# Moving the sample rows' normalisation and half of chunk 1's projection inside a retention head

## What is computed

```python
h = rmsnorm(x, g_mix)
u, q, k, v, ga, gb = jnp.split(h @ w_in, IN_SPLITS, axis=-1)
pool_out, new_hist = pool_mixer(u, pool_hist, pool_valid, w_pool, pool_scale)
qf = rotary(q, pos); kf = rotary(k, pos) * RET_DK ** -0.5
ret, s_new = retention(qf, kf, v, ret_state)          # 4 heads, chunks of 128 rows
ret_out = head_group_norm(ret, ret_gn)                # (o - mean) * rsqrt(var + EPS) per row and head
mixed = sigmoid(ga) * pool_out + sigmoid(gb) * ret_out
x = x + mixed @ w_out
x = x + hier_moe(rmsnorm(x, g_ffn))                   # 32 experts, two for each row
```

## Time and profile before

| | us |
|---|---|
| median of 3 runs (1114.18 to 1115.68) | 1114.87 |
| the profiled execution, whole | 1117.15 |
| its span, first to last instruction | 1115.0 |
| PE busy in the span | 1018.3 (91%) |
| DVE busy in the span | 758.4 (68%) |
| ACT busy in the span | 441.9 (40%) |
| mean granted TensorE clock | 0.965 |

### The profile page before, as it was taken

The page is one execution under the profiler, slowest core; times in us unless marked ns, Lnnn a source line. Parts: engine busy times, 40 slices in busy tenths (PEclk is TensorE's granted clock), DMA queues, the critical chain, the costliest instruction groups (busy, mean ns, idle before and its releaser), DMA issues.

```text
span 1115.0 us, 17147 instructions
## 1 busy us (share of the span) xinstructions
PE 1018.3 (91%) x5426; PEld 866.0 (78%) x5427; DVE 758.4 (68%) x1846; ACT 441.9 (40%) x733; POOL 211.3 (19%) x227
## 2 busy tenths in 40 slices
PE   5799999899998999999998999968999999998980
PEld 5788887888888888788885888856887877777860
DVE  5674556746557455574566667668998989878964
ACT  6521113011130111301112211235988888877964
POOL 0001220012200122001221000002423333345310
PEclk9899999999999999999998999988999999999995
DMA  8511016010060010610107433288999999999728
GB/s 253 201 31 55 11 40 195 2 40 28 23 194 21 24 44 13 190 34 24 44 11 259 157 134 115 113 322 346 352 384 387 377 375 361 376 361 344 244 34 311
DMA packets 74736, 190.36 MB, mean 171 GB/s; under 512 B 12504, under 2 KB 47556, under 8 KB 62228
## 3 DMA queue, kind: packets, MB, share of 16 engines
q1 hardware_dynamic: 61403, 159.66, 38.7%
q0 software_dynamic: 13248, 29.62, 9.5%
HBM read 167.43 MB, written 38.68 MB: 185 GB/s over the span
## 4 chain that ended last, share of the span: by engine, by line
PE 61%; DMA 23%; DVE 9%; issue 4%; ACT 1%; SPq 1%; POOLq 0%; POOL 0%; DVEq 0%; ACTq 0%
DMA sum_d<-y,icol 18%; PE bank L1788 16%; PE bank L1789 8%; PE bank L848 8%; PE bank L821 6%; PE bank L823 5%; PE bank L822 5%; DMA xg<-h_d,icol 2%; DVE line L1999 2%; PE bank L877 1%; PE bank L1810 1%; PE bank L1802 1%; PE bank L1798 1%; PE bank L1685 1%; DMA hc<-const_head_tables_dram 1%
## 5 line engine op out<-in xcount | busy, mean ns | idle before, releaser
L1194 DVE TENSOR_TENSOR w_lo<-w,w_hi 128x1024 fp32r<-128x1024 f32 x128 | 150.6, 1217 | 0.7 <-ACT w_hi L711 0.2
L711 ACT ACTIVATE w_hi<-w 128x1024 fp32r<-128x1024 f32 x128 | 129.5, 1068 | 4.3 <-PE bank L823 4.3
L1788 PE MATMUL bank<-wvg_hi,hT_hi 128*128 128x512 f32 x288 | 117.0, 406 | 0.0
L1638 ACT ACTIVATE v<-bank 128x256 f32<-128x256 f32 x36 | 13.8, 383 | 252.6 <-PE bank L1789 252.6
L1788 PE MATMUL bank<-wvg_lo,hT_hi 128*128 128x512 f32 x288 | 113.5, 394 | 0.0
L1788 PE MATMUL bank<-wvg_hi,hT_lo 128*128 128x512 f32 x288 | 113.2, 393 | 0.0
L821 PE MATMUL bank<-w_hi,xT_hi 128*128 128x512 f32 x256 | 103.8, 405 | 3.2 <-DVE xT_lo L1205 1.5
L821 PE MATMUL bank<-hT_hi,wuqk_hi 128*128 128x344 f32 x288 | 97.4, 338 | 8.7 <-DVE qT L1975 6.9
L823 PE MATMUL bank<-w_hi,xT_lo 128*128 128x512 f32 x256 | 100.9, 394 | 0.0
L822 PE MATMUL bank<-w_lo,xT_hi 128*128 128x512 f32 x256 | 100.4, 392 | 0.0
L822 PE MATMUL bank<-hT_lo,wuqk_hi 128*128 128x344 f32 x288 | 94.2, 327 | 0.0
(11 more groups left out here) (231 smaller groups left out, 2380.2 us busy)
## 6 DMA issues: line engine op xcount, KB each, us to landing
w<-in_w_dram SPq DMA_DIRECT2D x96, 1024.0 KB
raw<-in_w_in_dram SPq DMA_DIRECT2D x60, 256.0 KB, 3.2
xall<-in_x_prompt_dram SPq DMA_DIRECT2D x8, 512.0 KB, 7.1
mixed_d<-mixed POOLq DMA_DIRECT2D x32, 128.0 KB, 2.2
sample_state<-in_state_ret_dram SPq DMA_DIRECT2D x16, 256.0 KB, 3.8
out_dram<-sample_state SPq DMA_DIRECT2D x16, 256.0 KB, 3.7
mixed_in<-mixed_d SPq DMA_DIRECT2D x8, 512.0 KB, 4.4
x_again<-in_x_prompt_dram SPq DMA_DIRECT2D x8, 512.0 KB, 3.3
```

What stands on the lines that cost most here:

```text
L711: act.activation(hi, whole_w, ACT.Copy).then_inc(S["up_hi"], 1)
L1194: dve.tensor_tensor(lo, whole_w, hi, ALU.subtract).then_inc(S["up_lo"], 1)
L1788: g = pe.matmul(gates, x[xi], wvg[wi][:, 1:3, k, :], start=first, stop=last)
```

## The change

`finish(h - 1, CH)` leaves the end of `tail` and stands behind the first rotation of the next head, n = 3. `finish_rest(h - 1, CH)` moves from behind rotation 3 to behind rotation 6. Behind head 3 both keep their place. On PE, the projection of chunk 1 is cut in two: its first four k steps are issued ahead of `before(1)`, the other four behind it. The number of instructions of each kind stays the same, and no buffer changes.

```diff
-                def project(c):
-
-                    if c == 0:
-                        pe.wait_ge(S["w_lo"], after(18 * h + 18))
-                    if c >= 2:
+                def project(c, ks=range(KT)):
+
+                    if ks[0] > 0:
+                        pass
+                    elif c >= 2:
                         pe.wait_ge(S["sig_done"], after(9 * h + c - 1))
                         pe.wait_ge(S["v_ev"], after(9 * h + c - 1))
                     else:
+                        if c == 0:
+                            pe.wait_ge(S["w_lo"], after(18 * h + 18))
                         pe.wait_ge(S["s_upd"], after(4 * h))
                         pe.wait_ge(S["qk_ev"], after(6 * h + 5 + c))
...
-                    for k in range(KT):
+                    for k in ks:
...
-                    g.then_inc(S["g_mm"], 1)
-                    m.then_inc(S["v_mm"], 1)
+                    if ks[-1] == KT - 1:
+                        g.then_inc(S["g_mm"], 1)
+                        m.then_inc(S["v_mm"], 1)
...
                 for c in range(NT):
                     if c == 0:
                         project(0)
-                    before(c)
-                    if c > 0:
+                        before(0)
+                    elif c == 1:
+                        project(1, range(0, 4))
+                        before(1)
+                        project(1, range(4, KT))
+                        attend(0)
+                    else:
+                        before(c)
                         project(c)
-                    if c > 0:
                         attend(c - 1)
...
                     between(g)
-                finish(h, CH)
-                assert steps.n - n == per_tail - NEWTON, steps.n - n
+                assert steps.n == n
...
                     if n == 3 and not first:
+                        finish(h - 1, CH)
+                    if n == 6 and not first:
                         finish_rest(h - 1, CH)
...
             tail(H - 1, lows)
+            finish(H - 1, CH)
             finish_rest(H - 1, CH)
```

## The result

The changed kernel has a median of 1097.27 us (4 runs, 1097.07 to 1098.83) against 1115.14 us (4 runs, 1114.18 to 1115.68): a ratio of 0.9846, interval 0.9825 to 0.9867, so 17.9 us less. Forecast were 13.5 us less, 1101.4, with a range down to 1098.5.

The account below looks back on a forecast made before the run. PE was taken to bound the heads, its waits costing more than their idle time. DVE's part 6.9 plus PE's part 6.6 gave 13.5 us, carried in full to the end: 1114.87 to 1101.4 us, range 1098.5 to 1107.

Parts of the forecast that it names:

- What bounds, and what a wait costs: Heads: PE bounds, busy 1018.3 of 1115.0 us; each rotation wait costs 0.25 us over its idle time.
- The rival that only idle time comes back: Heads: time beside the stops is work that goes elsewhere, so gain only 10.0 us, 1104.9; chance 12%.
- the start-to-start sums: Waits counted by instruction starts: in head 1, projection 5's costs 1.20 us, projection 6's 1.83.
- DVE's part: Heads 1 to 3: six rotation waits worth 8.4 us go, three new waits of 0.5 come; gain 6.9 us.
- The new wait: PE at `project(0)` waits for rotation 7 behind `finish_rest`: 0.5 us in each of three heads, bounds 0 to 1.1.
- `finish` at 2.31: DVE behind rotation 3: `finish` takes 2.31 us from its gate product to the copy, stops included.
- the slack of 1.0: Head 1: rotation 4 ready at 193.7, projection 6 wants it at 194.7, so that wait goes with 1.0 us to spare.
- PE's part: Chunk 1's projection cut in two around `before(1)`: mask and key waits go in four heads; gain 6.6 us.
- The cover of 4.2 us: Half of chunk 1's projection runs ahead of `before(1)`, bringing PE there at about 219.8, after the mask at 217.1.
- the two undisturbed `before` and the extra break: PE time that must stay: 0.25 us for each `before` and 0.08 for one more projection break, per head.
- The way to the end: Behind head 3: stage C moves forward whole with the heads, despite DMA at 1.00, so the full gain is carried.
- the rival on the slow side: Stage C falls out of step: 32 expert additions each 0.5 us longer lose 16 us, 1117.4; chance 4%.

Follow-up runs that it names:

- the experiment with both halves at rotation 3: Changed kernel with `finish_rest` directly behind `finish`, both behind rotation 3; sample update to first key transpose 46.50, 45.87 and 45.76 us in heads 1 to 3.
- PE's delay of 14.4 us: Changed kernel with 132 needless PE transposes in head 0, so stage C begins as late as before the change; 1119.58 us (11 runs).
- the three comparisons: Changed kernel, unedited, against the kernel before, three times: 1097.27 against 1115.14, 1105.05 against 1116.09, 1102.72 against 1117.71 us.
- the pair with plain writes: Kernel before and changed kernel, both with the experts' adding indirect DMA replaced by one that only writes: 1101.34 and 1088.80 us.
- the cut behind one k step: Changed kernel with chunk 1's projection cut after its first k step; first key transpose to that of chunk 2: 10.79, 10.94, 10.92, 10.77 us.

## Why the prediction was wrong, and where it was right

**What bounds, and what a wait costs: right.** A wait costs more than its idle column says. PE's stretch shows it best: 6.45 us gained over the four heads, and the idle time that went was 3.5 + 1.1 = 4.6. The rival that only idle time comes back (10.0 us in all) falls: the heads gave 13.7. Nor did more come back than the stops: in head 1 of the changed kernel 1.20 + 1.83 - 0.34 = 2.7 us were to go by the start-to-start sums, and 2.4 to 2.6 went; the granted clock of that stretch is 1.00 before and after.

**DVE's part: right, 7.3 for 6.9.** Rotation 3 was ready in time, `finish` fitted in, `finish_rest` took 5.65 from rotation to rotation. The new wait was forecast at 0.5 and costs about 0.34. Its other term, `finish` at 2.31, was mis-sized by 0.4 to 0.6, which the slack of 1.0 hid here and the experiment with both halves at rotation 3 laid open.

**PE's part: right, 6.45 for 6.6.** The cover of 4.2 us was more than enough, the two undisturbed `before` and the extra break cost what was said.

**The way to the end: right for the gain, wrong for the range.** The first expert load moved with the heads, from 728.89 to 714.38, 14.5 us:

```profile
714.38 6.79 SPq L503 DMA_DIRECT2D w<-in_w_dram  x4
```

and PE's delay of 14.4 us cost 14.5.

The step that failed is the term for the scatter between executions, above all that of stage C. I took it from three runs that differ by 1.5 us ("0.05 an expert"), used it only against the rival on the slow side, and left it out of the bounds; "about 0.2% (2.2 us)" for what a measurement can tell is too small in the same way. Experts 11 to 32 alone took 214.03 and 211.09 us in two traces of the kernel before, and 210.09, 216.13 and 211.43 in three of the changed one: 6 us apart, or nearly 0.3 an expert. All runs of the kernel before together (62) have a median of 1116.3 us and a standard deviation of 2.9; those of the changed kernel (16) 1102.7 and 3.6. With these a comparison of four runs with four has a standard error of sqrt(2.9^2 / 4 + 3.6^2 / 4) = 2.3 us and can miss the true gain by 4.6, two of them. The pooled medians are 13.6 us apart, the three comparisons 17.9, 11.0 and 15.0, the pair with plain writes 12.5. So I take the change to be worth 13.7 us in the stretches that it touches, and some 4 us of the first comparison's 17.9 to be luck; in the profiled pair they are 0.96 ahead of the heads and 3.94 in experts 11 to 32. That is argued from the later comparisons and not shown of the first: its own interval, 14.8 to 19.5 us, does not hold 13.7, while the other two (9.7 to 15.4, 11.4 to 18.0) do.

**What stays open.** From the start of the heads to the third group of L834 the mean gain is a little smaller, 12.5 us: 570.77, 571.56 and 570.24 in the traces of the kernel before (the last with plain writes) against 557.23, 557.60, 559.91 and 558.53 of the changed one. The missing 1.2 don't lie in the head starts. The four of them sum to 36.2 us in the three traces of the kernel before and to 36.0 in the four of the changed one, so nothing was lost there, although the readouts' idle wait for the sample states is longer (1.7 to 1.8 us in all against 2.4 to 3.7). Longer in the mean, by 1.2, is the way from where the last head start ends to the third group of L834: 22.7, 21.3 and 21.2 us before, 22.9, 22.4, 23.7 and 22.7 changed. But that way takes from 19.3 to 24.1 us over all thirteen traces, so whether PE's earlier arrival costs something there or scatter does was not settled.

That the 4 us are scatter and no effect of the change rests on the later comparisons; the first eight runs themselves lie closely together (1.5 and 1.8 us), which independent draws with a deviation of 2.9 and 3.6 would rarely do, and each kernel has only one trace from that time. A gain of 17.9 that holds on the chip of those first runs alone is not excluded. Why later runs of either kernel spread over 6 to 15 us was not settled. They come from other chips or another time, and nothing here tells chip from time.

## What to carry to other kernels

When two engines hand a bank to and fro, write down start-to-start times for both and move the work of the late one into a gap that follows a hand-over; count a stall from start to start, since its idle time is only part of it. A cover has to reach to the event that is waited for, not just exist. Before giving a range, ask which stretch of the kernel sets the scatter between executions: three runs that lie close together don't measure it, while two traces of one kernel, cut at the same points, show at once where some of it sits.

## What the runs showed of the hardware

In the last 22 experts it is the adding form of the indirect DMA that sets the pace; the share of DMA time does not tell it. With plain writes the share is still 1.00, PE has no gap from 775 to 1000 us, and the stretch falls from 209 to 216 us to 197.7 (197.74 and 197.73). What in the adding costs the time was not taken apart. The Trainium skill (Perfetto Trace Analysis, Identifying the Most-Contended Engine) warns that occupancy is misleading for DMA; this case's 1.00 with and without a bound agrees.

The granted clock falls now and then at a head's start, where PE has short matmuls and waits, and it differs between executions. The windows run from the first sample update to the end of the projection behind it: head 2 of the changed kernel, then head 3 of its third trace.

```profile
297.23:304.30 7.07, 5.95 (x32) 5.16 (x33) 4.18 (x21) 1.90 (x3) 1.03 (x2) 1.00 0.43 136
```

```profile
436.33:446.22 9.89, 8.58 (x33) 7.79 (x33) 7.74 (x26) 1.90 (x3) 1.29 (x2) 0.65 0.55 161
```

The same instructions take 7.07 us at the 2.4 GHz level and 9.89 at a mean of 0.65, that is, mostly at 1.2. The starts of heads 2 and 3 scatter from 8.2 to 11.5 us over all traces but that of the late stage C (12.2), a wider span than what either part of the change gains in a head. The granted clock sorts them. Of the fourteen in the table, the three with a mean clock of 0.69 or 0.70 over the start take 11.1 to 11.3 us, the nine at 0.82 or 0.83 take 9.5 to 10.2, and the two at 1.00, 9.45 and 9.77, have a readout that waits 0.8 and 1.1 us. At 1.00 and without such a wait the start of head 3 took 8.19 us, in the trace of the cut behind one k step. The start of head 1 is at 1.00 in all thirteen traces and takes 7.39 to 7.41.
